# Sixteen experts on one core: tokens' rows sorted through DRAM and turned on TensorE, heads moved around a turning, two gate rows by transfer

## What is computed

```python
def _moe(h, w_router, b_router, w1, w3, w2):
    scores = jax.nn.sigmoid(h @ w_router)                 # 256 tokens x 16 experts
    ...                                                   # best of 4 groups, then the best 2 in it
    gates = jnp.sum(jax.nn.one_hot(idx, N_EXPERTS) * wts[..., None], axis=1)
    for e in range(N_EXPERTS):                            # D = 1024, FF = 512
        he = jax.nn.silu(h @ w1[e]) * (h @ w3[e])
        out = out + gates[:, e:e + 1] * (he @ w2[e])
```

```python
def ab_layer(x, xc, mod, mod_c, ...):
    h, gate = adaln(x, mod)                               # rmsnorm(x) * (1 + scale) + shift; gate: 1024 numbers
    hc, gate_c = adaln(xc, mod_c)
    qa, ka, va, qb, kb, vb, g = heads_ab(h @ w_in, ...)   # latent heads (a), grouped heads (b)
    qac, kac, vac, qbc, kbc, vbc, gc = heads_ab(hc @ w_in, ...)
    ...
    x = x + gate * (mix @ w_out)
    xc = xc + gate_c * (mixc @ w_out)
```

## Time and profile before

| | before |
|---|---|
| median of 3 runs | 1002.72 us (1002.15 to 1007.28) |
| profiled execution | 1004.23 us |
| its span | 1002.4 us |
| TensorE matmul (PE) busy | 942.2 us, 94% |
| TensorE weight load (PEld) busy | 513.4 us, 51% |
| DVE busy | 373.4 us, 37% |
| ACT busy | 308.4 us, 31% |
| POOL busy | 31.7 us, 3% |
| moved by DMA | 230.75 MB, mean 230 GB/s |

### The profile page before, as it was taken

One profiled execution on the slowest core, in us unless ns is written; L12 is line 12 of the kernel. 1 busy time (PEld: TensorE's weight loads), 2 busy tenths in 40 slices (PEclk: granted clock), 3 DMA queues, 4 the chain that ended last, 5 costly groups with the idle time before them and its releaser, 6 DMA issues.

```text
span 1002.4 us, 11949 instructions
## 1 busy us (share of the span) xinstructions
PE 942.2 (94%) x4380; PEld 513.4 (51%) x4381; DVE 373.4 (37%) x838; ACT 308.4 (31%) x700; POOL 31.7 (3%) x54
## 2 busy tenths in 40 slices
PE   3899989999999899997999999999989999999998
PEld 1455446546454335442355446455766456577763
DVE  1200497634271110522122321610855633236452
ACT  3211533332131121342233321311466632125420
POOL 0100200000000000000000002000000000000000
PEclk9999999999999999999999999999989999999999
DMA  9966482489696699899799999414226734423501
GB/s 349 364 212 229 50 314 99 157 297 336 215 365 229 216 334 393 297 396 396 276 398 383 398 396 295 178 48 157 85 84 239 215 93 168 161 91 101 133 19 42
DMA packets 105693, 230.75 MB, mean 230 GB/s; under 512 B 3124, under 2 KB 6504, under 8 KB 105496
## 3 DMA queue, kind: packets, MB, share of 16 engines
q1 hardware_dynamic: 100288, 217.85, 61.5%
q0 software_dynamic: 2208, 7.37, 2.6%
q10 hardware_dynamic: 3128, 4.62, 1.4%
HBM read 224.31 MB, written 5.51 MB: 229 GB/s over the span
## 4 chain that ended last, share of the span: by engine, by line
PE 84%; DVE 5%; ACT 4%; DMA 4%; issue 2%; SPq 1%; ACTq 0%; DVEq 0%
PE bank L633 24%; PE bank L900 12%; PE bank L647 9%; PE bank L913 6%; PE bank L930 4%; PE bank L599 3%; PE bank L1208 3%; DMA arena<-in_w_mod_dram 3%; PE bank L1137 3%; PE bank L1227 2%; PE bank L1218 2%; PE bank L829 1%; PE bank L925 1%; PE bank L762 1%; PE bank L983 1%
## 5 line engine op out<-in xcount | busy, mean ns | idle before, releaser
L633 PE MATMUL bank<-arena 128*128 128x512 f32 (+3 forms) x592 | 236.6, 558 | 1.9 <-DVE arena L2687 1.0
L633 PEld LDWEIGHTS bank<-arena 128*128 128x128 f32 x592 | 111.2, 190 | 117.9 <-issue 109.1
L900 PE MATMUL bank<-arena 128*64 128x512 f32 x512 | 113.0, 593 | 3.4 <-issue 3.4
L647 PE MATMUL bank<-arena 128*128 128x256 f32 (+1 forms) x384 | 99.3, 417 | 2.8 <-ACT arena L1935 1.5
L647 PEld LDWEIGHTS bank<-arena 128*128 128x128 f32 x384 | 72.1, 190 | 30.9 <-issue 21.7
L900 PEld LDWEIGHTS bank<-arena 128*64 128x64 f32 x512 | 38.8, 137 | 73.9 <-issue 73.3
L913 PE MATMUL bank<-arena,con 128*64 128x512 f32 x272 | 65.0, 621 | 4.6 <-ACT con L1838 4.0
L599 PE MATMUL bank<-arena,silu_c 128*32 128x512 f32 x384 | 48.8, 630 | 9.5 <-DMA arena<-in_w_mod_dram 6.7
L1739 ACT ACTIVATE con<-bank 128x256 f32<-128x256 f32 x17 | 6.5, 383 | 137.3 <-PE bank L900 137.3
L2358 DVE TENSOR_TENSOR con<-con,bank 128x256 f32<-128x256 f32 x17 | 7.2, 421 | 109.5 <-ACT con L1743 109.5
L913 PEld LDWEIGHTS bank<-arena,con 128*64 128x64 f32 x272 | 21.4, 143 | 37.6 <-issue 36.5
(11 more groups left out here) (409 smaller groups left out, 1209.8 us busy)
## 6 DMA issues: line engine op xcount, KB each, us to landing
arena<-in_w_gate_e_dram SPq DMA_DIRECT2D x16, 2048.0 KB, 14.0
arena<-in_w_up_e_dram SPq DMA_DIRECT2D x16, 2048.0 KB, 13.6
arena<-in_w_down_e_dram SPq DMA_DIRECT2D x16, 2048.0 KB, 12.4
arena<-in_w_mod_dram SPq DMA_DIRECT2D x12, 2048.0 KB, 12.0
arena<-in_mod_w_dram SPq DMA_DIRECT2D x12, 2048.0 KB, 8.0
arena<-in_ab_w_in_dram SPq DMA_DIRECT2D x7, 2048.0 KB, 9.6
arena<-in_gla_w_in_dram SPq DMA_DIRECT2D x6, 2048.0 KB, 11.1
arena<-in_cd_w_in_dram SPq DMA_DIRECT2D x6, 2048.0 KB, 7.9
```

The lines of the kernel that those rows point to most:

```text
L633: mm = pe.matmul(ps[:, 0:n], lhs[:, k, tile * P:(tile + 1) * P], w[:, k, c0:c0 + n], start=(k == 0), stop=(k == kd_ - 1))
L647: mm = pe.matmul(ps[:, i * n:(i + 1) * n], w[:, k, c * P:(c + 1) * P], rhs[:, k, 0:n], start=(k == 0), stop=(k == KC - 1))
L900: mm = pe.matmul(up_b[64 * j:64 * j + 64, :], h[:, k, :], blocks[:, g + n:u + n + 1:u - g, :], start=(k == 0), stop=(k == KC - 1), tile_po ...
```

## The change

**Sorting.** The 448 further selection rows and the 16 matmuls of `gather` are dropped. DVE casts the places to integers right after the 64-place rows. POOL writes the tokens' rows into their places in a DRAM tensor `h_rows` by four indirect transfers (128 rows each), waits for all four, and reads the 448 rows behind the first 64 back with two transfers into a free slot (`sorted_rows`). TensorE turns them (`turn_sorted`, 8 chunks of three 128-column transposes and one of 64), and this stands behind expert 0's down, no longer ahead of its turning. The evictions by ACT and DVE move behind expert 0's store and product. POOL's `ctx_line`, and a new line for `gate(2)`'s numbers, are issued behind the read-back.

**Heads.** At expert 5 the grouped heads of both tiles are turned into three banks in place of four, the second tile's queries follow ahead of the turning, and its keys stand between turning and down. Before, both stood behind the down. At expert 7 the second tile's turned heads stand ahead of the turning and the first scores behind it; before, the heads stood behind expert 6's down.

**Gate rows.** `gate(2)` and `gate(3)` are dropped on all engines. POOL writes the numbers as lines to DRAM and reads them back with a broadcast, as it does for the context. It issues `gate(2)`'s read once the squares of a context tile's latents are there and `gate(3)`'s once 12 products have been added.

```diff
@@ DVE, places
-            for lo, hi in GATHERED:
-                for t in range(TT):
-                    places_in, row = iota[:, lo:hi], sel[:, t, lo:hi]
-                    link(dve.tensor_scalar(row, places_in, slots_ab[:, t, 0:1], None, ALU.is_equal))
-                    dve.scalar_tensor_tensor(row, places_in, slots_ab[:, t, 1:2], row, ALU.is_equal, ALU.add)\
-                       .then_inc(sel_ready, 1)
+            for t in range(TT):
+                row = sel[:, t, :]
+                link(dve.tensor_scalar(row, iota[:, 0:CAP], slots_ab[:, t, 0:1], None, ALU.is_equal))
+                dve.scalar_tensor_tensor(row, iota[:, 0:CAP], slots_ab[:, t, 1:2], row, ALU.is_equal, ALU.add)\
+                   .then_inc(sel_ready, 1)
+            dve.tensor_copy(route_idx[:, :, :], slots_ab).then_inc(slots_ready, 1)
...
-            dve.tensor_copy(route_idx[:, :, :], slots_ab)
@@ POOL
+            pool.wait_ge(slots_ready, 1)
+            for t in range(TT):
+                for j in range(2):
+                    pool.indirect_dma_start(out=h_rows, out_offset=bass.IndirectOffsetOnAxis(ap=route_idx[:, t, j:j + 1], axis=0),
+                                            in_=xn2[:, t, :], in_offset=None).then_inc(rows_out, 16)
+            pool.wait_ge(rows_out, 16 * 4)
+            banks.wait(pool, "first5")
+            pool.dma_start(sorted_rows[:, 0:3, :], h_rows[CAP:CAP + 3 * P, :].rearrange("(t p) d -> p t d", p=P))\
+                .then_inc(rows_back, 16)
+            pool.dma_start(sorted_rows[0:2 * T - CAP - 3 * P, 3, :], h_rows[CAP + 3 * P:2 * T, :]).then_inc(rows_back, 16)
             pool.wait_ge(modcol_ready, 18)
             pool.dma_start(ctx_line.rearrange("(c p) -> p c", p=P), mod2[:, 0, 16:24, 1],
                            allow_slow_non_contiguous=True).then_inc(ctx_line_out, 16)
+            pool.dma_start(gate_lines[0].rearrange("(c p) -> p c", p=P), mod2[:, 0, 16:24, 0],
+                           allow_slow_non_contiguous=True).then_inc(ctx_line_out, 16)
@@ TensorE, turning in place of gathering
-            def gather(other_branch=False):
-                pe.wait_ge(sel_ready, 2 * TT)
+            def turn_sorted(other_branch=False):
+                pe.wait_ge(rows_back, 16 * 2)
                 for k in range(KC):
...
-                    for t in range(TT):
-                        mm = pe.matmul(ps[:, 0:2 * T - CAP], xn2[:, t, k * P:(k + 1) * P], sel[:, t, CAP:2 * T],
-                                       start=(t == 0), stop=(t == TT - 1))
+                    for i in range(4):
+                        n = P if i < 3 else 2 * T - CAP - 3 * P
+                        mm = pe.transpose(ps[:, i * P:i * P + n], sorted_rows[0:n, i, k * P:(k + 1) * P], ident[0:n, 0:n])
                     banks.filled(name, mm)
...
                         ctx_latents(6)
-                        gather(True)
                         behind_up(e)
+                        turn_sorted(True)
@@ ACT and DVE: evictions of gather() behind expert 0's store and product
             for e in range(NE):
                 i, b = e // 2, e % 2
-                if e == 0:
-                    act.wait_ge(hg_v, 1)
-                    gather()
-                else:
+                if e:
...
                 store(y_buf[b], slot0, stored[b])
                 if e == 0:
+                    gather()
                     extras(e)
@@ fill work
-                    5: [("gT", 2), ("gT", 3)], 6: [("hT", 2)]}
-        CTX_WORK_TURNED = {3: [("cT", 3)]}
-        CTX_WORK_BEHIND = {5: [("heads", 3)], 6: [("hT", 3)]}
+                    5: [("gT", 0), ("qa", 3)], 6: [("hT", 2)]}
+        CTX_WORK_TURNED = {3: [("cT", 3)], 5: [("kv", 3)]}
...
-            CTX_WORK[e] = ([("turns", g - 1)] * (g > 0) + [("scores", g)] * (g < 8)
+            CTX_WORK[e] = ([("turns", g - 1)] * (g > 0) + [("scores", g)] * (0 < g < 8) + [("hT", 3)] * (g == 0)
                            + [("gate", n) for n in range(2) if CTX_GATES_AT[n] == e])
-            CTX_WORK_TURNED[e] = [("values", g - 1)] * (g > 0)
+            CTX_WORK_TURNED[e] = [("values", g - 1)] * (g > 0) + [("scores", 0)] * (g == 0)
@@ gate rows: POOL, at its end; DVE waits for them
+            pool.wait_ge(qk_ms, NORM_AT["latent", 2] + 1)
+            pool.dma_start(gate_rows[:, 0, :], gate_lines[0].partition_broadcast(P)).then_inc(gate_row_in, 16)
+            pool.wait_ge(modcol_ready, 24)
+            pool.dma_start(gate_lines[1].rearrange("(c p) -> p c", p=P), mod2[:, 1, 16:24, 0],
+                           allow_slow_non_contiguous=True).then_inc(ctx_line_out, 16)
+            pool.wait_ge(ctx_line_out, 48)
+            pool.wait_ge(y_added, 12)
+            pool.dma_start(gate_rows[:, 0, :], gate_lines[1].partition_broadcast(P)).then_inc(gate_row_in, 16)
...
-            dve.wait_ge(gate_bc, 6)
+            dve.wait_ge(gate_row_in, 16)
...
-            dve.wait_ge(gate_bc, 8)
+            dve.wait_ge(gate_row_in, 32)
```

76 lines of the change are left out of this document (37 added, 39 removed).

## The result

The changed kernel takes 1020.1 us (median of 4 runs, 1017.05 to 1024.72) against 1005.0 for the kernel before (4 runs): a ratio of 1.0153, 95% interval 1.0122 to 1.0184. It is slower by 1.5%, and the forecast was 993.6 and faster. The profiled execution took 1017.05 us, its span is 1015.3, 12.9 more than before (the medians are 15.1 apart). Of these, 3.05 arise ahead of everything that the change touches: expert 0's up begins at 305.35 and not 302.30. All that follows is counted from expert 0's up.

A forecast was written before the change was run, and what follows sets the result against it. TensorE, 84% of the chain that ended last, was taken to bound the kernel. Front 3.5, heads 2.3 and gate rows 3.3 sum to 9.1 us: 995.1 from 1004.23, 993.6 against the median 1002.72; range 990.0 to 1000.5.

The forecast's parts named there:

- The front: Expert 0's up to expert 1's context columns: scatter, read-back and transposes replace gathering, 3.5 us less, bounds 0 and 6.8.
- the turning and the start of the down: Expert 0, once gathering is gone from TensorE's path: turning at 317.8, down at 318.8.
- The scatter is slow: Rival, chance 0.08: TensorE and POOL's copy wait for the rows; 0.5% slower if back from 339.8, 1007.9 us at 340.
- Late rows: Rival, chance 0.15: expert 2's loads go first, read-back at 333.0, front loses 3.7 us; time 1000.8.
- Transposes: Behind expert 0's down: 32 transposes of the sorted rows take 3.9 us, from sixteen taking 1.95.
- The clock: Rival, chance 0.17: the clock falls after idles at up 1, expert 1's fill or down 7, 1.7 us each; time 996.5.
- the wait of 3.3 for the weights: TensorE waits from 335.7 to 339.0 for the context weights that open expert 1's fill.
- Heads: Heads and turnings of experts 5 to 7 fill waits or leave the loop: 2.3 us less, bounds 0.8 and 2.5.
- its up would start at 461.64 - 2.6 = 459.0: Expert 8: its up weights land at 459.2, the load that limits what the heads can save.
- Gate rows: Near 783 and 870, TensorE loses two pairs of 512-column matmuls: 3.3 us less, bounds 2.0 and 3.7.
- The wait for ACT: At the gate rows: ACT keeps its other work, so a wait for it may return part of the gain.
- What would show it wrong: Signs: long idle ahead of transposes, read-back after 329, late loads at experts 6 to 8, or a wait for gate rows.

The follow-up runs named there:

- lines turned: Changed kernel with heads as before (1.9: heads of the change, 1000.79 us); TensorE turns both lines, written in 512-byte pieces ahead of the scatter: 998.83 us, ratio 0.9956.
- no sorting: Kernel before with the change's heads and gate rows but the gathering matmuls of before, both lines written at 298 us: 1005.3 us, ratio 1.0029.
- one line late: Changed kernel with only the first gate line moved to the end of the experts, the context's line left behind the read-back: 1018.0 us, ratio 1.0129.
- with the first gap filled: Kernel with TensorE-turned lines written early, plus three idle matmuls ahead of expert 0's turning: 1000.26 us, ratio 0.9962.

## Why the prediction was wrong

**The front: one term was left at nothing.** The step that failed is "The ctx line and gate line (1024 elements each) are issued behind the read-back, ahead of expert 1's copy; POOL is free again some 2 us after the read-back". It priced the two lines by POOL's time to issue them. POOL was free by 314, as written; the DMA engines were not. Each line costs the front 7 to 9 us, and without them (lines turned, written early) the turning and the start of the down come out within 0.2 us, and the context weights land at 339.4 where 339.0 was worked out. There was a hint to be read. In the trace of before, the same context line of 4 KB (KB, us to landing) took longer than the 8.2 of a 2 MB load:

```profile
ctx_line<-mod POOLq DMA_DIRECT2D x1, 4.0 KB, 11.7
```

TensorE lost nothing by it there: from 300 to its landing at 306.6 DMA moved only 9 GB/s, and expert 1's weights were not wanted until 335. The change moved it into the loads and doubled it.

**Its rivals.** "The scatter is slow" (0.08) gave the right sign by the wrong mechanism: the scatter took 8.0. "Late rows" named the right place (read-back done about 330, weights after), but by service in order of issue; with the lines out of the way the read-back takes 9.0 beside the same loads, so the queues do share. The Trainium skill ("DMA: Bandwidth & Descriptors", "Queues, rings and completion order") has a DMA engine take turns between its queues. The clean front agrees: the read-back takes 9.8 from its first issue to its last landing, between 6.7 alone and 11.4 at half share by the prediction's figures, and the load beside it 12.6 in place of 8.3. The Trainium skill's page "DMA: Bandwidth & Descriptors" also says, under "Rules for kernel authors", that a last dimension that is not contiguous goes as one descriptor per element, and to rearrange it. That rule speaks against the two lines and I did not weigh it; the runs agree that rearranging pays (17.5 us against 8.0 for the same 4 KB), while the descriptors themselves do not show in the trace.

**Terms of the front that were mis-sized.** Transposes: 3.9 from sixteen of 96 partitions, measured 5.51 at full clock for 32 of 128 and 64. The clock: two falls, in down 0 and up 1, took 1.4 and 1.7 even in the clean front, and the sum had none. TensorE then comes to the context columns 4.7 later than forecast; the wait of 3.3 for the weights, which the sum did have, falls away, and the front is worth 2.0 and not 3.5. That it comes near is therefore partly luck: the wait that was to set it did not occur. In times, sorting with clean lines and gate rows (0.9956) cannot be told from gate rows alone (0.9945); that the sorting gains anything is read from the profile alone and stays open.

**Heads: the wrong sign.** The step that failed is "These loads stand back to back in a full queue and don't move relative to expert 5's up." The keys ahead of expert 5's down move that down, and the down frees a slot: one load is asked for 5.2 later. Besides, "its up would start at 461.64 - 2.6 = 459.0", just behind the load, left out that 2.1 to 2.2 us pass at this place between a landing that TensorE waits for and its first matmul (the program reads a flag and branches in between). In before, the pass began at 461.44, 2.2 behind its load (459.2), so hardly anything could be gained there. (The sum's own savings give 2.5, not 2.6, and 461.64 is the end of the down ahead of that pass; neither matters here.) Forecast 2.3 less; the profiled stretch from expert 5's up to the last expert's is 1.2 (the change), 1.3 (no sorting) and 1.9 (lines turned) longer. Falls of the clock move that stretch by more, 182.7 to 187.0 us with the heads of before and 184.3 to 191.3 with those of the change, so what is shown is the later load and that the gain did not come, not the size of the loss.

**Gate rows**: 3.3 forecast, 4.0 in the profile, and 0.9945 by themselves. The wait for ACT that I had allowed for did not come.

**What would show it wrong** named "the read-back landing after 329" and "loads that come late at experts 6 to 8"; both came.

## What to carry to other kernels

Price a transfer by its pieces, not by its bytes or by the time it takes to issue: 4 KB in single numbers cost this front 7 to 9 us, more than a load of 2 MB (5.3 at 393 GB/s), even where only the source has them apart, and the cost falls on the loads beside it. Turn or copy such a vector first (pieces of 32 bytes were long enough here), or write it while no loads run. And where a step is moved ahead of the last reader of a weight slot, follow the slot: in a full queue the load behind it, not the idle that was filled, sets the time.

## What the runs showed that was not expected

The number of pieces is set by the source as well: contiguous in DRAM but 8 bytes apart in the source, a line landed after 17.5 us; contiguous on both, after 8.0. From a landing to the first matmul of TensorE that waits for it, with a flag to read and a branch in between, 1.3 to 1.5 us passed at expert 7's up and 2.1 to 2.2 at expert 8's second-round pass, which has a second flag and branch. And a fall of the clock that moves: with the first gap filled, the down ran at full clock, and the low stretch behind the second gap was longer (up 1 at 9.66 in place of 8.78). It did not come behind every such gap: with one line late, up 1 took 7.09 behind the same 2.49 us of idle.
